# Hybrid decoder layer on one core: the residual reload ahead of a wait, sums of squares in column quarters, inverse roots spread by transposes

## The chip, the cores and the metric

The kernel runs on one core of a Trainium2 chip. The metric is the device time of one execution in microseconds (us). It is 1467.88 us, the median of three runs (1467.37 to 1468.05).

## The reference

One decoder layer over 1024 tokens of width 1024, with 16 learned meta tokens ahead of them, all in float32:

```python
u = rmsnorm(h, norm1_g)
proj = u @ w_in                        # q, k, v of 8 attention heads; q, f, i, g of 4 recurrent heads
o_sb = stick_breaking_attention(...)   # A[t,s] = sigmoid(z_ts) * prod_{s<j<t} (1 - sigmoid(z_tj))
o_sb = group_rmsnorm(merge_heads(o_sb), sb_norm_g, SB_HEADS)
o_hg = hgrn2_chunkwise(...)            # gated linear recurrence in chunks of 128
o_hg = group_rmsnorm(merge_heads(o_hg), hg_norm_g, HG_HEADS) * jax.nn.silu(hg_g)
h = h + jnp.concatenate([o_sb, o_hg], axis=-1) @ w_out
u2 = rmsnorm(h, norm2_g)
h = h + (jax.nn.silu(u2 @ w_gate) * (u2 @ w_up)) @ w_down
```

A last rmsnorm and the cut of the meta tokens follow. `group_rmsnorm` divides each head's output by the root of its mean square over the head's own width (64 in attention, 128 in the recurrence).

## The kernel before

Everything is written out by hand: each engine has its own instruction stream, and semaphores tie them. Large products are done with split operands: a float32 tensor is kept as a high part (fp32r) and a low part, and a product is three matmuls (high by high, high by low, low by high), lines 268 to 270 for results with features on the partitions and lines 280 to 282 for results with tokens on the partitions. The order of the stages is norm 1 and projections (to about 83 us), the recurrence of four heads (to about 351 us, `recurrence_tensor`), attention by four pairs of heads (to about 623 us, `attention_tensor`), the output projection with the residual sum and norm 2 (to about 746 us), and the FFN (to the end).

Head outputs lie with features on the partitions, so a head's mean square is a sum over partitions, and it is done on TensorE. Each half of a head (recurrence) or of a pair (attention) makes one group of four 128x128 tiles:

- Sums. ScalarE writes the squares; TensorE loads each tile of squares as weights and streams a column of ones (recurrence, `unit_sums`, line 576) or two columns that pick out the two heads of a pair (attention, `head_norm_tensor`, line 965). The result has tokens on the partitions.
- Roots. ScalarE takes the square root (line 979 in attention), VectorE inverts it and widens it to a tile (`widen`, and `head_norm_widen`, lines 986 and 988).
- Spread. TensorE loads the widened tile as weights and streams the identity (`unit_spread`, line 585, and line 971), which turns it so that tokens are on the columns. VectorE then scales `mixed` with it (line 807, and `head_norm_finish`, line 996).

There are 8 such groups in the recurrence and 8 in attention, so 16 groups of sums and 16 of spreads. The plain float32 matmuls of these lines appear as two instructions each in the trace.

Attention works on 56 pieces (14 for each pair of heads; a piece is a stretch of keys of one block of 128 queries). For each piece TensorE makes scores (lines 901 and 905), ScalarE two sigmoids (1029, 1032), VectorE a scan and a product (1084, 1091), TensorE turns the two heads' weights (917), two copies bring them out of PSUM, and TensorE multiplies by the values (936). The first head's copy is on ScalarE (line 1056). The second is on VectorE (line 1103) for pieces 0 to 41, and on ScalarE (line 1059) from piece 42, which is `SCALAR_COPIES`. In the last pair VectorE and ScalarE also split `mixed` into high and low parts (lines 1010 and 1015, at the pieces of `SPLIT_AT`; piece 53 is the last of them).

At the end of attention the last half goes out of PSUM (lines 1039 and 1040, semaphore `av_evac`), then through sums, root, spread, and scaling (semaphore `s_mixed`, value 8), while TensorE has begun the output projection. `out_group(c, t)` is 24 matmuls for column chunk `c` of 256 and token tile `t`; it uses one of four PSUM banks, so the fifth group waits for the first residual sum (`o_add`), and it also waits for the last split (`m_lo`, 16). The residual sum is `add` on VectorE (line 1351), into `h_res`, which is loaded again from `x` by GpSimd's queue. The queue's order is:

```python
pool.wait_ge(s_mixed.sem, s_mixed.done(8))
pool.dma_start(gain[:], norm2_g[0:1, :].to_broadcast([P, D])).then_inc(gain2.sem, 16)
pool.wait_ge(av_evac.sem, av_evac.done(8))
for t in range(TT):
    pool.dma_start(h_res[:, t, :], x2[t * P:(t + 1) * P, :]).then_inc(x_back.sem, 16)
```

`gain` shares its memory with the squares and the widened roots of attention. `h_res` lies over attention's inputs, which are no longer read once `av_evac` has its eighth count. VectorE waits for all eight tiles (`x_back` at 128) ahead of the first `add`.

Of the kernel before, what the change touches and what calls it, by code (L numbers as in the profile page):

```python
# [12 lines left out]
P = 128  # L13
# [5 lines left out]
TT = SEQ // P  # L19
# [57 lines left out]
PER_PAIR = len(PIECES) // 4  # L77
# [56 lines left out]
def hybrid_layer(nc, x, meta, norm1_g, w_in, sb_g, hg_g, lb_logits, w_out, norm2_g,  # L134
                 w_gate, w_up, w_down, final_g, out):
    x2, out2 = x[0], out[0]
# [7 lines left out]
    with ctx:  # L144
# [3 lines left out]
        def signal(name, credit=0):  # L148
            return Signal(ctx.enter_context(nc.semaphore(name)), credit)


        ident = sb("ident", [P, P])
        ident_bf = sb("ident_bf", [P, P], BF16)
        hidden_bf = sb("hidden_bf", [P, P], BF16)
        ones = sb("ones", [P, P])
        ones_pair = sb("ones_pair", [P, 2])
# [23 lines left out]
        with ExitStack() as heads:  # L180
# [7 lines left out]
            with ExitStack() as hg:  # L188
# [20 lines left out]
                scores = sb("scores", [P, U], stack=hg)  # L209
                kd_nat = sb("kd_nat", [P, U], stack=hg)  # L210
# [5 lines left out]
        squares, spread = gain[:, 0:HALF], gain[:, HALF:2 * HALF]  # L216
        gate_buf = (g_even[:], gain[:])

        with ExitStack() as ff:
# [5 lines left out]
            h_res = sb("h_res", [P, TT, D], stack=ff)  # L225
# [6 lines left out]
        def bank(n, w=HALF, rows=P):  # L232
            return ps[0:rows, n * HALF:n * HALF + w]
# [3 lines left out]
        META_COLS = slice(SEQ, L)  # L237
        MIX_HG = SB_WIDTH // P
        KEY_HALVES = [slice(0, P // 2), slice(P // 2, P)]
        UNITS = [(h, half) for h in range(HG_HEADS) for half in range(2)]  # L240


# [70 lines left out]
        av_done, av_evac = signal("av_done"), signal("av_evac")  # L313
# [1 line left out]
        s_inv, s_wide, s_spread = signal("s_inv"), signal("s_wide"), signal("s_spread")  # L315
        s_mixed = signal("s_mixed")
        m_hi, m_lo = signal("m_hi"), signal("m_lo")
        x_back, gain2, gain3 = signal("x_back"), signal("gain2"), signal("gain3")
        o_proj, o_add = signal("o_proj"), signal("o_add")
        came = {c: signal(f"w{c}_came") for c in "gud"}  # L320
        high = {c: signal(f"w{c}_high") for c in "gud"}
# [201 lines left out]
        def unit_scores(pe, n):  # L523
            head, half = UNITS[n]
            par = head % 2
# [46 lines left out]
        def unit_sums(pe, n):  # L572

            pe.wait_ge(h_square.sem, h_square.done(n + 1))
            for c in range(UNIT):
                last = nc.tensor.matmul(bank(4)[:, 2 * P + c:2 * P + c + 1],
                                        (kd_nat, scores)[n % 2][:, c * P:(c + 1) * P], ones[:, 0:1],
                                        start=True, stop=True)
            last.then_inc(h_sum.sem, 1)

        def unit_spread(pe, n):

            pe.wait_ge(h_wide.sem, h_wide.done(n + 1))
            for c in range(UNIT):
                last = nc.tensor.matmul(bank(1 + n % 2)[:, c * P:(c + 1) * P],
                                        (kd_nat, scores)[n % 2][:, c * P:(c + 1) * P], ident[:],
                                        start=True, stop=True)
            last.then_inc(h_spread.sem, 1)

        def meta_transpose(pe, head):  # L590
# [277 lines left out]


        NP = len(PIECES)  # L870
        SCALAR_COPIES = 3 * PER_PAIR

        def filling(n):

# [86 lines left out]
        def head_norm_tensor(pe, e, step, psum):  # L961
            if step == "sums":
                pe.wait_ge(s_square.sem, s_square.done(e + 1))
                for c in range(UNIT):
                    last = nc.tensor.matmul(psum[:, 2 * c:2 * c + 2], squares[:, c * P:(c + 1) * P],
                                            ones_pair[:], start=True, stop=True)
                last.then_inc(s_sum.sem, 1)
            else:
                pe.wait_ge(s_wide.sem, s_wide.done(e + 1))
                for c in range(UNIT):  # L970
                    last = nc.tensor.matmul(psum[:, c * P:(c + 1) * P], spread[:, c * P:(c + 1) * P], ident[:],
                                            start=True, stop=True)
                last.then_inc(s_spread.sem, 1)

        def head_norm_scalar(act, e, psum):
# [45 lines left out]
        def attention_scalar(act):  # L1021
            def sigmoids(n):
                pair, b, lo, hi, width, buf = PIECES[n]
                w, cols = hi - lo, place_of(n)
                act.wait_ge(z_done.sem, z_done.done(n + 1))
                if last_user(n) is not None:
                    act.wait_ge(t_done.sem, t_done.done(2 * last_user(n) + 2))
                for par in range(2):
                    nc.scalar.activation(beta[:, par, buf, cols], bank(2 * par + n % 2, w), ACT.Sigmoid,  # L1029
                                         scale=-SB_SCALE).then_inc(beta_done.sem, 1)  # L1030
                for par in range(2):
                    nc.scalar.activation(probs[:, par, buf, cols], bank(2 * par + n % 2, w), ACT.Sigmoid,
                                         scale=SB_SCALE).then_inc(sig_done.sem, 1)

            def out_evac(e):
                act.wait_ge(av_done.sem, av_done.done(e + 1))
                if e:
                    act.wait_ge(s_sum.sem, s_sum.done(e))
                nc.scalar.activation(squares, bank(5), ACT.Square).then_inc(s_square.sem, 1)
                nc.scalar.activation(mixed[:, e // 2, X_PARTS[e % 2]], bank(5), ACT.Copy).then_inc(av_evac.sem, 1)  # L1040

            def evacuate_filled(n):
                for j, u, piece in filling(n):
                    if piece != 0:
                        evacuate(act, j, u)

            evacuate(act, HG_HEADS + 1, "q0")
            act.wait_ge(h_mixed.sem, h_mixed.done(2 * HG_HEADS))
            sigmoids(0)
            sigmoids(1)  # L1050
            for n in range(NP):
                if n + 2 < NP:
                    sigmoids(n + 2)
                w = P * len(tiles_of(n))
                act.wait_ge(t_done.sem, t_done.done(2 * n + 1))
                nc.scalar.activation(probs_t[:, 0, 0:w], bank(4, w), ACT.Copy).then_inc(pt_first.sem, 1)
                if n >= SCALAR_COPIES:
                    act.wait_ge(t_done.sem, t_done.done(2 * n + 2))
                    nc.scalar.activation(probs_t[:, 1, 0:w], bank(6, w), ACT.Copy).then_inc(pt_second.sem, 1)
                if n in SUMS_AT:  # L1060
                    head_norm_scalar(act, SUMS_AT[n], bank(n % 2)[:, HALF - 8:HALF])
                evacuate_filled(n)
                if n - 1 in HALF_ENDS:
                    out_evac(HALF_ENDS.index(n - 1))
                for part in range(2):
                    if n - part in CHUNK_AT:
                        high_chunk(act, CHUNK_AT[n - part], None, part)
                for t, half in SPLIT_AT.get(n, []):
                    split_scalar(act, t, half)
            out_evac(7)  # L1070

        def attention_vector(dve):
# [24 lines left out]
            for n in range(NP):  # L1097
                w = P * len(tiles_of(n))
                if n in SPREAD_AT:
                    head_norm_finish(dve, SPREAD_AT[n], bank(7))  # L1100
                if n < SCALAR_COPIES:
                    dve.wait_ge(t_done.sem, t_done.done(2 * n + 2))
                    nc.vector.tensor_copy(probs_t[:, 1, 0:w], bank(6, w)).then_inc(pt_second.sem, 1)
                if n - 1 in SUMS_AT:
                    head_norm_widen(dve, SUMS_AT[n - 1])
                if n + 2 < NP:
                    weigh(n + 2)
                for part in range(2):
                    if n - 1 - part in CHUNK_AT:
                        low_chunk(dve, CHUNK_AT[n - 1 - part], part)  # L1110
                for t, half in SPLIT_AT.get(n, []):
                    split_vector(dve, t, half)


        with nc.Block() as blk:
# [45 lines left out]
            def _(pool):  # L1161
# [32 lines left out]
                for h in LEVELS[1:]:  # L1194
                    last = nc.gpsimd.memset(fac[h][:], 1.0)
                last.then_inc(fills.sem, 1)
                pool.wait_ge(s_mixed.sem, s_mixed.done(8))
                pool.dma_start(gain[:], norm2_g[0:1, :].to_broadcast([P, D])).then_inc(gain2.sem, 16)
                pool.wait_ge(av_evac.sem, av_evac.done(8))
                for t in range(TT):  # L1200
                    pool.dma_start(h_res[:, t, :], x2[t * P:(t + 1) * P, :]).then_inc(x_back.sem, 16)
                pool.wait_ge(n2.normed.sem, n2.normed.done(TT))
                pool.dma_start(gain[:], final_g.rearrange("(a n) -> a n", a=1).to_broadcast([P, D]))\
                    .then_inc(gain3.sem, 16)
# [104 lines left out]
            def _(dve):  # L1309
# [36 lines left out]

                def add(c, t):

                    dve.wait_ge(o_proj.sem, o_proj.done(TT * c + t + 1))
                    h = h_res[:, t, c * CW:(c + 1) * CW]  # L1350
                    nc.vector.tensor_tensor(h, h, bank(out_bank(c, t), CW), ALU.add).then_inc(o_add.sem, 1)  # L1351
# [3 lines left out]
                    hi_, lo_ = slot or ffn_slot(c)  # L1355
                    nc.vector.tensor_tensor(lo_, w_raw[:], hi_.bitcast(F32), ALU.subtract).then_inc(low[c].sem, 1)

                dve.wait_ge(x_back.sem, 16 * TT)
                for c in range(4):
                    for t in range(TT):  # L1360
                        add(c, t)
# [220 lines left out]
```

## Time and profile before

| | |
|---|---|
| median of three runs | 1467.88 us |
| profiled execution, its own time | 1466.36 us |
| its span, first to last instruction | 1464.3 us |
| TensorE busy, share of the span | 96% |
| VectorE, ScalarE, GpSimd busy | 50%, 30%, 1% |
| mean granted TensorE clock | 0.994 of full |
| chain of work that ended last: TensorE's share | 91% |

The trace is one execution. PE is TensorE's matmuls, PEld its weight loads, DVE is VectorE, ACT ScalarE, POOL GpSimd. L1351 is line 1351 of the kernel. Matmuls overlap each other in the pipeline, so the time from one start to the next says more than the duration of one. A query of the chain gives what each piece of time was waited on for; a query of waits gives idle time of an engine and who ended it.

### The profile page before, as it was taken

What the parts mean: (1) busy time and instruction counts of PE and PEld (TensorE: products, weight loads), DVE (VectorE), ACT (ScalarE), POOL (GpSimd) and SP (SyncE); (2) the same over time, 40 slices, a digit from 0 to 9 for tenths busy, and PEclk for the clock granted to TensorE, in tenths of its full rate; (3) what the DMA queues carried; (4) which work ended last, traced back from release to release, by engine and by line L of the source; (5) the groups of instructions that cost most, each with busy time, mean ns of one, the idle gap of its engine ahead of it and who ended that gap; (6) DMA issues with size and microseconds to landing.
All of it is one profiled execution on the core that took longest, in us unless ns stands there. A gap on an engine that the chain in (4) does not pass through costs nothing.

```text
span 1464.3 us, 20834 instructions
## 1 busy us (share of the span) xinstructions
PE 1401.8 (96%) x8732; PEld 1190.4 (81%) x8732; DVE 738.0 (50%) x1178; ACT 440.6 (30%) x770; POOL 20.3 (1%) x48
## 2 busy tenths in 40 slices
PE   5999999998999999769999999999999999999998
PEld 5898989897777777569987888888888888888886
DVE  6476677763776565812542435252533425152437
ACT  6323322223665556811432112111111112121113
POOL 3000000000000000010000000000000000000000
PEclk9999999999999999989999999999999999999999
DMA  6211111010010000040121011020201111020202
GB/s 189 58 30 30 30 30 53 22 44 0 1 59 1 30 2 30 1 158 30 58 73 58 29 58 58 29 87 0 86 23 63 31 55 57 29 86 0 86 0 115
DMA packets 61194, 68.78 MB, mean 47 GB/s; under 512 B 1584, under 2 KB 54832, under 8 KB 61120
## 3 DMA queue, kind: packets, MB, share of 16 engines
q1 hardware_dynamic: 59408, 61.94, 13.2%
q0 software_dynamic: 1712, 5.78, 1.1%
q8 instruction: 56, 0.92, 0.3%
q14 instruction: 18, 0.15, 0.0%
HBM read 63.51 MB, written 4.19 MB: 46 GB/s over the span
## 4 chain that ended last, share of the span: by engine, by line
PE 91%; ACT 5%; DMA 1%; issue 1%; DVE 1%; POOL 0%; ACTq 0%; DVEq 0%; POOLq 0%
PE ps L268 18%; PE ps L269 18%; PE ps L270 18%; PE ps L1542 16%; PE ps L936 3%; PE ps L917 2%; PE ps L280 2%; PE ps L282 2%; PE ps L281 2%; PE ps L901 2%; PE ps L549 2%; PE ps L384 1%; DMA h_res<-in_x_dram 1%; ACT bv L503 1%; ACT beta L1029 1%
## 5 line engine op out<-in xcount | busy, mean ns | idle before, releaser
L268 PE MATMUL ps<-a_hi,w_hi 128*128 128x512 f32 (+2 forms) x960 | 357.0, 372 | 8.5 <-DVE a_lo L376 2.9
L269 PE MATMUL ps<-a_lo,w_hi 128*128 128x512 f32 (+2 forms) x960 | 349.6, 364 | 0.0
L270 PE MATMUL ps<-a_hi,w_lo 128*128 128x512 f32 (+2 forms) x960 | 349.3, 364 | 0.0
L268 PEld LDWEIGHTS ps<-a_hi,w_hi 128*128 128x128 f32 x960 | 181.4, 189 | 33.8 <-DVE a_lo L376 3.3
L270 PEld LDWEIGHTS ps<-a_hi,w_lo 128*128 128x128 f32 x960 | 181.4, 189 | 23.4
L269 PEld LDWEIGHTS ps<-a_lo,w_hi 128*128 128x128 f32 x960 | 181.6, 189 | 22.1
L1386 DVE TENSOR_TENSOR silu<-silu,ps 128x512 f32<-128x512 f32 x44 | 30.2, 687 | 319.1 <-ACT silu L1272 319.1
L1398 DVE TENSOR_TENSOR h_res<-h_res,ps 128x512 f32<-128x512 f32 x176 | 116.3, 685 | 48.0 <-PE ps L1542 47.9
L1272 ACT ACTIVATE silu<-ps 128x512 f32<-128x512 f32 x44 | 26.4, 600 | 337.2 <-PE ps L270 337.2
L268 PE MATMUL ps<-a_hi,d_hi 128*128 128x512 f32 x320 | 124.5, 389 | 0.0
L269 PE MATMUL ps<-a_lo,d_hi 128*128 128x512 f32 x320 | 124.5, 389 | 0.0
L1542 PE MATMUL ps<-w_hi,f_hi 128*128 128x512 f32 x320 | 124.5, 389 | 0.0
L1542 PE MATMUL ps<-w_lo,f_hi 128*128 128x512 f32 x320 | 124.5, 389 | 0.0
L1542 PE MATMUL ps<-w_hi,f_lo 128*128 128x512 f32 x320 | 124.5, 389 | 0.0
L270 PE MATMUL ps<-a_hi,d_lo 128*128 128x512 f32 x320 | 124.5, 389 | 0.0
L1084 DVE TENSOR_TENSOR_SCAN beta<-beta,ones 128x272 f32<-128x272 f32 (+5 forms) x112 | 92.9, 871 | 15.8 <-ACT beta L1029 15.8
L1253 ACT ACTIVATE w_hi<-w_raw 128x2048 fp32r<-128x2048 f32 x22 | 42.2, 1920 | 167.0 <-DMA w_raw<-in_w_up_dram 67.7
L280 PE MATMUL ps<-w_hi,a_hi 128*128 128x256 f32 x256 | 74.1, 290 | 12.2 <-DVE h_res L1351 10.8
L435 DVE TENSOR_TENSOR w_lo<-w_raw,w_hi 128x2048 fp32r<-128x2048 f32 (+1 forms) x22 | 41.8, 1901 | 65.7 <-ACT w_hi L417 65.6
L281 PE MATMUL ps<-w_lo,a_hi 128*128 128x256 f32 x256 | 73.3, 286 | 0.0
L282 PE MATMUL ps<-w_hi,a_lo 128*128 128x256 f32 x256 | 73.3, 286 | 0.0
L268 PEld LDWEIGHTS ps<-a_hi,d_hi 128*128 128x128 f32 x320 | 60.2, 188 | 12.5
(193 smaller groups left out, 1959.8 us busy)
## 6 DMA issues: line engine op xcount, KB each, us to landing
w_raw<-in_w_in_dram SPq DMA_DIRECT2D x24, 512.0 KB
w_raw<-in_w_gate_dram SPq DMA_DIRECT2D x11, 1024.0 KB, 5.1
w_raw<-in_w_up_dram SPq DMA_DIRECT2D x11, 1024.0 KB, 5.2
w_raw<-in_w_down_dram SPq DMA_DIRECT2D x11, 1024.0 KB, 5.0
mixed<-in_x_dram SPq DMA_DIRECT2D x8, 512.0 KB, 7.3
w_raw<-in_w_out_dram SPq DMA_DIRECT2D x4, 1024.0 KB
h_res<-in_x_dram POOLq DMA_DIRECT2D x8, 512.0 KB, 8.0
out_dram<-h_sq SPq DMA_DIRECT2D x8, 512.0 KB, 2.6
```

What stands on the lines that cost most here:

```text
L268: nc.tensor.matmul(psum, wh, ah, start=k == 0, stop=False)
L269: nc.tensor.matmul(psum, wh, al, start=False, stop=False)
L270: last = nc.tensor.matmul(psum, wl, ah, start=False, stop=k == KT - 1)
L280: nc.tensor.matmul(psum, ah, wh, start=n == 0, stop=False)
L281: nc.tensor.matmul(psum, ah, wl, start=False, stop=False)
L282: last = nc.tensor.matmul(psum, al, wh, start=False, stop=n == KT - 1)
L435: last = nc.vector.tensor_tensor(w_lo[:, s, c], w_raw[:, c], w_hi[:, s, c].bitcast(F32), ALU.subtract)
L936: last = nc.tensor.matmul(dst, v, probs_t[:, par, i * P:(i + 1) * P], start=hi == width and i == 0, stop=lo == 0 and i == len(tiles) - 1)
L1084: nc.vector.tensor_tensor_scan(c, c, ones[:, 0:1].to_broadcast([P, hi - lo]), begin, ALU.mult, ALU.mult).then_inc(scanned.sem, 1)
L1253: nc.scalar.activation((slot or ffn_slot(c))[0], w_raw[:], ACT.Copy)\
L1398: nc.vector.tensor_tensor(h, h, bank(4 + g % 4), ALU.add).then_inc(dn_add.sem, 1)
L1542: last = nc.tensor.matmul(bank(4 + g % 4), fa[:, par, f, a], dw[:, w], start=f == 0 and m == 0, stop=f == 1 and m == 2)
```

## The change

There are five edits.

1. On GpSimd's queue the eight loads of `h_res` come first, behind `av_evac` alone; the gain of norm 2 comes behind them, after its wait for `s_mixed`.
2. `x_back` becomes one semaphore for each token tile, and `add(0, t)` waits for its own tile.
3. The sums of squares (both `unit_sums` and `head_norm_tensor`) are made by four matmuls for each tile in place of one: each loads 32 columns of the squares and writes 32 partitions of PSUM.
4. The spreads (both) are TensorE transposes in place of float32 matmuls by the identity.
5. `SCALAR_COPIES` becomes the range of pieces 42 to 53, so the second copies of pieces 54 and 55 go to VectorE.

```diff
+        QUARTERS = [slice(32 * i, 32 * i + 32) for i in range(4)]
@@
-        x_back, gain2, gain3 = signal("x_back"), signal("gain2"), signal("gain3")
+        x_back = [signal(f"x_back{t}") for t in range(TT)]
+        gain2, gain3 = signal("gain2"), signal("gain3")
@@ unit_sums
-                last = nc.tensor.matmul(bank(4)[:, 2 * P + c:2 * P + c + 1],
-                                        (kd_nat, scores)[n % 2][:, c * P:(c + 1) * P], ones[:, 0:1],
-                                        start=True, stop=True)
+                for rows in QUARTERS:
+                    last = nc.tensor.matmul(bank(4)[rows, 2 * P + c:2 * P + c + 1],
+                                            (kd_nat, scores)[n % 2][:, c * P + rows.start:c * P + rows.stop],
+                                            ones[:, 0:1], start=True, stop=True)
@@ unit_spread
-                last = nc.tensor.matmul(bank(1 + n % 2)[:, c * P:(c + 1) * P],
-                                        (kd_nat, scores)[n % 2][:, c * P:(c + 1) * P], ident[:],
-                                        start=True, stop=True)
+                last = nc.tensor.transpose(bank(1 + n % 2)[:, c * P:(c + 1) * P],
+                                           (kd_nat, scores)[n % 2][:, c * P:(c + 1) * P], ident[:])
@@
-        SCALAR_COPIES = 3 * PER_PAIR
+        SCALAR_COPIES = range(3 * PER_PAIR, NP - 2)
@@ head_norm_tensor
-                    last = nc.tensor.matmul(psum[:, 2 * c:2 * c + 2], squares[:, c * P:(c + 1) * P],
-                                            ones_pair[:], start=True, stop=True)
+                    for rows in QUARTERS:
+                        last = nc.tensor.matmul(psum[rows, 2 * c:2 * c + 2],
+                                                squares[:, c * P + rows.start:c * P + rows.stop],
+                                                ones_pair[:], start=True, stop=True)
@@
-                    last = nc.tensor.matmul(psum[:, c * P:(c + 1) * P], spread[:, c * P:(c + 1) * P], ident[:],
-                                            start=True, stop=True)
+                    last = nc.tensor.transpose(psum[:, c * P:(c + 1) * P], spread[:, c * P:(c + 1) * P], ident[:])
@@ attention_scalar
-                if n >= SCALAR_COPIES:
+                if n in SCALAR_COPIES:
@@ attention_vector
-                if n < SCALAR_COPIES:
+                if n not in SCALAR_COPIES:
@@ GpSimd's queue
+                pool.wait_ge(av_evac.sem, av_evac.done(8))
+                for t in range(TT):
+                    pool.dma_start(h_res[:, t, :], x2[t * P:(t + 1) * P, :]).then_inc(x_back[t].sem, 16)
                 pool.wait_ge(s_mixed.sem, s_mixed.done(8))
                 pool.dma_start(gain[:], norm2_g[0:1, :].to_broadcast([P, D])).then_inc(gain2.sem, 16)
-                pool.wait_ge(av_evac.sem, av_evac.done(8))
-                for t in range(TT):
-                    pool.dma_start(h_res[:, t, :], x2[t * P:(t + 1) * P, :]).then_inc(x_back.sem, 16)
@@ add(c, t)
+                    if c == 0:
+                        dve.wait_ge(x_back[t].sem, 16)
@@
-                dve.wait_ge(x_back.sem, 16 * TT)
```

## Rows read from the trace of the kernel before

**Rows 1.** Chain that ended last, 575 to 790 us: start, us, what

```profile
622.48 0.60 ACT mixed L1040
...
632.18 0.57 POOL gain L1198
632.75 3.65 POOL h_res L1201 x7
636.40 10.64 DMA h_res<-in_x_dram
```

**Rows 2.** Timeline of PE: start, us, engine line op out<-in tiles xcount [idle before <-releaser]

```profile
636.56 0.28 PE L282 MATMUL ps<-w_hi,a_lo 128*128 128x256 f32 x1
647.63 0.55 PE L280 MATMUL ps<-w_hi,a_hi 128*128 128x256 f32 x1 [10.79 <-DVE h_res L1351]
...
652.04 0.41 PE L282 MATMUL ps<-w_hi,a_lo 128*128 128x256 f32 x1
652.25 0.39 PE L280 MATMUL ps<-w_hi,a_hi 128*128 128x256 f32 x1
```

**Rows 3.** Busy by stage: PE, PEld, DVE, ACT, POOL, granted clock, DMA share, GB/s

```profile
647.00:655.00 8.00, 7.37 (x44) 7.40 (x44) 4.03 (x6) 0.00 (x0) 0.00 (x0) 0.66 0.38 131
```

**Rows 4.** Transfers of line 1201, whole span

```profile
DMA to landing us min/median/max: 5.4/8.0/10.6
```

**Rows 5.** Timeline of ACT and DVE after the last scaling

```profile
632.46 1.90 ACT L417 ACTIVATE w_hi<-w_raw 128x2048 fp32r<-128x2048 f32 x1
632.59 0.69 DVE L1015 TENSOR_TENSOR a_lo<-mixed,a_hi 128x512 fp32r<-128x512 f32 x1 [0.70 <-ACT a_hi L1010]
```

**Rows 6.** Timeline of PE, spread of the last half by float32 matmuls

```profile
630.04 1.06 PE L971 MATMUL ps<-ident,gain 128*128 128x128 f32 x8
...
630.86 0.36 PE L280 MATMUL ps<-w_hi,a_hi 128*128 128x256 f32 x1
```

**Rows 7.** Timeline of PE, eight transposes of norm 2

```profile
716.08 1.04 PE L384 MATMUL ps<-ident,h_norm 128*128 128x128 f32 x8
...
716.87 0.36 PE L280 MATMUL ps<-w_hi,a_hi 128*128 128x256 f32 x1
```

**Rows 8.** Timeline of PE, one group of sums in the recurrence

```profile
106.20 0.95 PE L576 MATMUL ps<-ones,kd_nat 128*128 128x1 f32 x8
...
107.01 0.40 PE L268 MATMUL ps<-a_hi,w_hi 128*128 128x336 f32 x1
...
107.25 0.32 PE L269 MATMUL ps<-a_lo,w_hi 128*128 128x336 f32 x1
```

**Rows 9.** Timeline of PE, one group of sums in attention

```profile
387.85 0.95 PE L965 MATMUL ps<-ones_pair,gain 128*128 128x2 f32 x8
388.73 0.30 PEld L901 LDWEIGHTS ps<-bf,bq 64*128 64x128 f32 x4
```

**Rows 10.** Timeline of PE, into column halves, through them, and out

```profile
83.27 0.60 PE L535 MATMUL ps<-ident,kd 128*128 128x128 f32 x4
83.80 1.09 PE L540 MATMUL ps<-bq,bk 128*64 128x128 f32 x16
84.72 0.64 PE L549 MATMUL ps<-mixed,bk 128*64 128x64 f32 x16
...
87.52 0.64 PE L549 MATMUL ps<-qd,kd 128*64 128x64 f32 x16
88.09 0.43 PE L268 MATMUL ps<-a_hi,w_hi 128*128 128x352 f32 x1
88.36 0.32 PE L269 MATMUL ps<-a_lo,w_hi 128*128 128x352 f32 x1
```

**Rows 11.** Chain that ended last, 585 to 623 us, its shares by line

```profile
by line: ACT a_hi L1010 18.9%; ACT probs_t L1059 13.5%; ACT beta L1029 13.4%; ACT probs_t L1056 11.8%; ACT probs L1032 10.6%; PE ps L936 9.8%; issue 6.7%; PE ps L917 3.9%; ACT L979 3.4%; ACT L1029 3.4%; ACT mixed L1040 2.9%; ACT gain L1039 
```

**Rows 12.** Timeline of ACT and DVE, second copy of piece 54

```profile
617.97 0.68 DVE L1015 TENSOR_TENSOR a_lo<-mixed,a_hi 128x512 fp32r<-128x512 f32 x1
618.03 0.49 ACT L1059 ACTIVATE probs_t<-ps 128x384 f32<-128x384 f32 x1
```

## Prediction

> **What bounds the kernel now.** The page comes first: TensorE is busy for 96% of the span and holds 91% of the chain that ended last, so time can be won where TensorE stops or where its work can be made shorter. The waits come next. TensorE stops for long at one place only, between attention and the FFN, and the chain through it reads as one story. The last attention output leaves PSUM at 622.48 + 0.60 = 623.08; GpSimd's queue is still waiting for the scaled last half and issues the norm gain at 632.18, then eight reloads from 632.75, and the last reload takes 10.64 us to land, until 647.04 [rows 1]. TensorE's last matmul before the stop starts at 636.56, the next at 647.63 [rows 2]. Its start to start there is normally 0.12 us, so the stop costs 647.63 - 636.68 = 10.95 us. Behind it the 256-column matmuls start every 0.21 us until 652.25 [rows 2]: 256 columns in 0.213 us is the lower of TensorE's levels, 1.2 GHz, and the stage's mean granted clock is 0.66 [rows 3]. That stretch of 4.62 us holds some 22 matmuls, which at 0.12 us take 2.6 us, so the idle engine's fallen clock costs 2.0 us more. The stop is worth 13.0 us in all.
>
> **Edits 1 and 2, the reload.** The loads can now issue from about 623.3 instead of 632.75 [rows 1], 9.4 us earlier, without the gain ahead of them (0.57 us). The first landed in 5.4 to 8.0 us and the last in 10.6 us after a start 3.7 us behind the first [rows 1, 4], so the first tile is there at about 629 to 631 and the last at 623.3 + 3.7 + 10.6 = 637.6. VectorE is free for the first add when its last split ends, 632.59 + 0.69 = 633.28 [rows 5]. The add of tile 0 then ends near 633.8, and TensorE asks for it at 636.68: 2.9 us to spare. Behind it on VectorE stands the split of the next weight chunk, which waits for ScalarE until 632.46 + 1.90 = 634.36 [rows 5] and ends near 636.7; the adds of tiles 1 to 3 follow, and TensorE asks for tile 1's bank one group (24 x 0.12 = 2.88 us) later, at 639.6. Nothing else is late, so the full stop and the slow stretch go: **-13.0 us**. The nine POOL issues keep their order but one: the gain now waits behind the reloads for 632.18 as before, is as large as one of them (0.5 MB, 5.4 to 10.6 us), and is wanted by norm 2 only near 716 us [rows 7]. VectorE's new waits by tile have a landed tile behind each. If the reload still came too late it would be by its last tile alone, 637.6 + 0.6 - 636.68 = 1.5 us of stop; I take 0.
>
> **Edit 4, transposes.** The spread of four tiles by float32 matmuls is eight instructions and takes 630.86 - 630.04 = 0.82 us [rows 6]. Eight transposes of the same tile size take 716.87 - 716.08 = 0.79 us [rows 7], and here eight instructions do eight tiles. Four will take about 0.42 with the 0.02 us that their first load starts late. Each group gets 0.40 us shorter. Of 16 groups, those of the recurrence (8) are all in TensorE's chain; of attention's 8, six are: from 585 to about 613 us the chain is ScalarE's [rows 11], and two spreads fall into it, where TensorE's time is not what is waited for. 14 x 0.40 = **-5.6 us**. The row of norm 2 is the same operation on the same tiles, so the bounds are close: 12 groups (-4.8) to all 16 (-6.4).
>
> **Edit 3, quarters.** Before, a group of sums has eight loads of 128 columns and takes 107.01 - 106.20 = 0.81 us up to the next matmul, whose successor comes after 0.24 us where 0.16 is normal for this width; 0.89 us with that [rows 8]. In attention it is 388.73 - 387.85 = 0.88 [rows 9]. The streams are one or two columns, so the load sets the 0.11 us between starts. Afterwards there are 16 matmuls, in float32 thus 32 instruction pairs, of 32 columns each. Two things have to be priced.
> Entering and leaving a narrower division of the array: the last full-width matmul starts at 83.27 + 3 x 0.11 = 83.61, and the first pair in halves at 83.80, where 0.11 later was due: 0.08 us, and a little more because the load no longer runs beside a matmul; I take 0.10. At the exit the last half starts at about 87.94 and the next at 88.09, 0.15 us, and the one behind it is late again (0.27 for 0.16), 0.11 us [rows 10]. In attention the score matmuls behind the sums use another division already, so that exit costs 0.18 before and after.
> The pair itself: in halves, 96 pairs go from 84.72 to 87.52, 0.029 us each, with 64 columns loaded and 64 streamed [rows 10]. That is the nearest row and the upper bound if nothing but width counts; the lower bound is the load alone with four quarters side by side, 0.112 / 4 / 4 = 0.007. I take 0.029, since nothing in the trace issues pairs faster.
> A group then costs 0.10 + 31 x 0.029 + 0.15 + 0.11 = 1.26 us in the recurrence (+0.37) and 0.10 + 0.90 + 0.18 = 1.18 in attention (+0.30). Eight of the first kind and seven of the second are in the chain (the eighth lies in the stretch that is ScalarE's): 3.0 + 2.1 = **+5.1 us**. At 0.007 it would be 8 x (0.58 - 0.89) + 7 x (0.50 - 0.88) = -5.1. The turning point is 0.018 us a pair.
> The Trainium skill's page TensorEngine Tiling (Array Packing), Instruction Overhead, speaks against this edit: a matmul costs about 60 cycles however few columns stream, and one should not tile a dimension that is already small. Its page TensorE: Matmul & The Clock Gate, in the part on 56 ns, puts the least start to start at about 25 ns; by that the quarters would cost +3.2 us and the sum would come 1.9 us lower. No row here streams fewer than 64 columns in a divided array, so the trace does not decide it.
>
> **Edit 5, the copies.** ScalarE's second copy of piece 54 ends at 618.03 + 0.49 = 618.52. VectorE is in the split of `mixed` until 617.97 + 0.68 = 618.65 [rows 12], so its copy ends about 0.49 later, 619.14, and TensorE's value matmuls and everything to the end of attention wait for it: **+0.6 us**. Were VectorE free, it would cost nothing; piece 55 is such a case, with a copy that starts and ends as before. Bounds 0 to 0.7.
>
> **The sum.** -13.0 - 5.6 + 5.1 + 0.6 = -12.9 us. Against the profiled execution (1466.36, of which 1464.3 is span) that is 1453.5; that execution was 1.5 us below the median of the runs, and the forecast for the median is 1467.88 - 12.9 = **1455.0 us**.
>
> **The rivals.**
> (a) Quarters are cheap: the pairs are not bound by the row of the halves, whose 64 streamed columns at 2.4 GHz alone take 27 ns. Then a pair costs 0.007 to 0.018 us, and the sum is 1467.88 - 13.0 - 5.6 + 0.6 - (0 to 5.1) = 1444.8 to 1449.9. For it: the halves' row is exactly its streaming time, so the load is not what limits it. Against it: 32 pairs are 64 instructions, and no row shows two instructions in less than 0.029. The page TensorE: Matmul & The Clock Gate of the Trainium skill, in the part on packing, gives about 4 ns from tile to tile, which is this rival.
> (b) A new wait stands in place of the stop: the reload's tiles land together at the end, or the split of the last half comes late because sums of 1.2 us lie ahead of it (slack 636.68 - 633.28 = 3.4 us, of which they take 0.3). That leaves 1.5 us of stop, and, if the clock falls again behind it, 2.0 us more: 1456.5 to 1458.5.
> (c) Slower than before: a 32-column load costs as much as a 128-column one, 0.112 us, and quarters are not taken side by side. The 15 groups in the chain then cost 465 x (0.112 - 0.029) = 38.6 us more than forecast, 1493.6. The point from which it decides is a pair of 0.029 + 12.9 / 465 = 0.057 us, which is what the halves take with 128 columns streamed (0.92 / 16 from 83.80 to 84.72) [rows 10]. Against it: the 0.029 of the halves is already far below.
>
> **How the numbers follow.** Forecast 0.60, (a) 0.28, (b) 0.09, (c) 0.03. The likeliest time is 1455.0, with its own range 1452 to 1457. For 8 times in 10 the range has to reach into (a), whose ends are even: 1446 to 1458. About 0.2% (2.9 us) is what a measurement of this kernel can tell from no change. All cases but (c) are faster by more: faster 0.96, same 0.01, slower 0.03.
>
> **What would show it.** In the changed kernel's profile: no wait of line 280 for `h_res`, the reload issued near 623, and a granted clock of 1.00 where it was 0.66; four instructions for a spread and about 0.42 us; 32 for a group of sums, whose start to start decides between forecast and (a) (above or below 0.018); the copy of piece 54 on VectorE starting at the end of the split of line 1015. Wrong would be: a stop of TensorE after the fourth group of the output projection, a spread of eight instructions, or a pair interval outside 7 to 29 ns.

## The result and the profile after

The changed kernel takes 1444.41 us (median of 4 runs, 1443.5 to 1445.05) where the kernel before takes 1467.62 (4 runs): a ratio of 0.9842, 95% interval 0.9825 to 0.9859, or 23.2 us less. Forecast were 12.9 us less and a range from 1446 to 1458. The result lies below the range, beside the lower end of rival (a).

The two profiled executions took 1466.36 and 1445.05 us, 21.3 us apart; the stages below are theirs. Five marks divide the span, each the start of an instruction: the first matmul of the recurrence's levels (line 549 before), the first scores of attention (line 901 before), the last copy out of attention's PSUM (line 1040 before), the first transposes of norm 2, and the end.

| stage, us | before | after | saved | forecast |
|---|---|---|---|---|
| norm 1 and projections, to line 549 | 84.7 | 85.6 | -0.9 | 0 |
| recurrence | 269.0 | 262.6 | 6.4 | 0.2 |
| attention | 268.8 | 267.0 | 1.8 | -0.4 |
| output projection, to norm 2's first transposes | 93.6 | 79.7 | 13.9 | 13.1 |
| norm 2 and the FFN | 748.2 | 748.2 | 0.0 | 0 |

(The last half of attention has its sums and its spread in the output projection; the forecast column is split that way.) No edit touches the first stage; in the other traces it takes 83.8 to 85.1 us. The reload came out as forecast. The surprise is in the recurrence.

First the reload. GpSimd's queue after (timeline; start, us, engine line, operation, idle before):

```profile
616.02 4.22 POOL L1202 DMA_DIRECT2D h_res<-in_x_dram  x8 [572.60 <-ACT mixed L1043]
624.03 0.53 POOL L1204 DMA_DIRECT2D gain<-in_norm_g_dram  x1 [3.79 <-DVE mixed L999]
```

The eight reloads issue right behind attention's last copy, and the gain behind them once the last half is scaled. On VectorE:

```profile
624.44 0.69 DVE L1018 TENSOR_TENSOR a_lo<-mixed,a_hi 128x512 fp32r<-128x512 f32 x1 [0.70 <-ACT a_hi L1013]
625.05 0.41 DVE L1356 TENSOR_TENSOR h_res<-h_res,ps 128x256 f32<-128x256 f32 x1
```

The first residual sum follows the last split without a gap, 9 us after the first reload was issued. By stages (PE, PEld, DVE, ACT, POOL busy, granted clock, DMA share, GB/s), where before stood [rows 3]:

```profile
616.00:632.00 16.00, 16.00 (x161) 15.85 (x162) 5.99 (x10) 3.73 (x4) 4.75 (x9) 1.00 0.90 339
632.00:695.00 63.00, 63.00 (x527) 63.00 (x526) 16.94 (x28) 8.65 (x9) 0.00 (x0) 1.00 0.15 50
```

TensorE is busy for 15.85 of the first 16 us and without a hole behind them, at full clock, although the DMA engines are 90% busy in the first. The stop of [rows 2] is gone, and no wait for `h_res` is left.

Now a group of sums in the recurrence, which answers to [rows 8] (PE's timeline):

```profile
106.88 0.32 PE L271 MATMUL ps<-a_hi,w_lo 128*128 128x352 f32 x1
107.13 0.43 PE L579 MATMUL ps<-ones,kd_nat 128*32 128x1 f32 x32
107.50 0.42 PE L269 MATMUL ps<-a_hi,w_hi 128*128 128x336 f32 x1
107.76 0.32 PE L270 MATMUL ps<-a_lo,w_hi 128*128 128x336 f32 x1
```

32 pairs take 107.50 - 107.13 = 0.37 us, way out included. The forecast had them at 0.90 without it. From the due start (106.88 + 0.16 = 107.04) to the second matmul behind it is 0.72 us; before, 106.20 to 107.25, it was 1.05. So the group got 0.33 us shorter where 0.37 longer was forecast. In attention:

```profile
382.15 0.32 PE L271 MATMUL ps<-a_hi,w_lo 128*128 128x336 f32 x1
382.40 0.43 PE L968 MATMUL ps<-ones_pair,gain 128*32 128x2 f32 x32
382.76 0.94 PE L903 MATMUL ps<-bf,bq 64*128 64x400 f32 x4
```

From the matmul ahead to the scores is 0.61 us, against 388.73 - 387.70 = 1.03 before ([rows 9]; the matmul ahead of that group started at 387.70): 0.42 less. The spread of the last half is four instructions and 0.36 us, against 0.82 in [rows 6]:

```profile
622.35 0.60 PE L975 MATMUL ps<-ident,gain 128*128 128x128 f32 x4
622.71 0.36 PE L281 MATMUL ps<-w_hi,a_hi 128*128 128x256 f32 x1
```

By these rows and the forecast's count of groups attention should have gained 6 x 0.42 + 5 x 0.40 = 4.5 us. It gained 1.8. Two questions were open: what a pair of quarters costs and why, and where 2.7 us of attention went.

### The profile page after: what moved, and what is told of

Read it like the earlier page. It is cut to its first block, busy times and chain, and to the rows that moved or that the text cites. A ratio compares the mean times of both kernels' runs of the same rounds, so it can differ in the third digit from the quotient of the medians.

```text
span 1443.0 us, 21481 instructions
## 1 busy us (share of the span) xinstructions
PE 1389.1 (96%) x9052; PEld 1172.3 (81%) x9052; DVE 739.0 (51%) x1180; ACT 439.2 (30%) x768; POOL 19.5 (1%) x48
## 3 DMA queue, kind: packets, MB, share of 16 engines
q1 hardware_dynamic: 59408, 61.94, 13.2%
## 4 chain that ended last, share of the span: by engine, by line
PE 93%; ACT 4%; DVE 1%; issue 1%; DMA 1%; ACTq 0%; DVEq 0%; POOLq 0%
PE ps L269 19%; PE ps L271 18%; PE ps L270 18%; PE ps L1546 17%; PE ps L938 3%; PE ps L919 3%; PE ps L281 2%; PE ps L283 2%; PE ps L282 2%; PE ps L903 2%; PE ps L551 2%; PE ps L386 1%; ACT bv L505 1%; PE ps L542 1%; DMA gain<-in_norm_g_dram 1%
## 5 line engine op out<-in xcount | busy, mean ns | idle before, releaser
L270 PE MATMUL ps<-a_lo,w_hi 128*128 128x512 f32 (+2 forms) x960 | 349.7, 364 | 0.0
L271 PEld LDWEIGHTS ps<-a_hi,d_lo 128*128 128x128 f32 x320 | 60.2, 188 | 12.6
```

The lines of the kernel that those rows point to most:

```text
L270: nc.tensor.matmul(psum, wh, al, start=False, stop=False)
L271: last = nc.tensor.matmul(psum, wl, ah, start=False, stop=k == KT - 1)
```

## The experiments

### One edit at a time

All four ran on one chip beside 25 runs of the kernel before (median 1466.60).

**Edits 1 and 2 alone.** (The lines of the queue; the semaphores by tile are those of the change.)

```diff
+                pool.wait_ge(av_evac.sem, av_evac.done(8))
+                for t in range(TT):
+                    pool.dma_start(h_res[:, t, :], x2[t * P:(t + 1) * P, :]).then_inc(x_back[t].sem, 16)
                 pool.wait_ge(s_mixed.sem, s_mixed.done(8))
```

> The kernel before with edits 1 and 2 alone (the reload first on GpSimd's queue, a semaphore for each tile). Theory (the stop of TensorE was a wait for the reload, and its slow stretch came with it): 13.0 us less than before, no wait of line 280 for h_res, granted clock 1.00 where it was 0.66. Rival (a new wait takes the stop's place): 9 to 11 us less.

Measured: 1453.29, ratio 0.9911 (0.9890 to 0.9931), 13.3 us less. The output projection is 13.2 us shorter in the trace (79.6 against 92.8 from its first matmul), all other stages as before, and TensorE has neither a stop nor a low clock:

```profile
636.00:656.00 20.00, 20.00 (x169) 20.00 (x169) 4.43 (x10) 1.92 (x1) 0.00 (x0) 1.00 0.23 80
```

This term of the sum is right. The stop and the low clock behind it went together, so the split into 11.0 and 2.0 us was not tested by itself.

**Edit 3 alone.** (Attention's lines; the recurrence's change likewise.)

```diff
-                last = nc.tensor.matmul(psum[:, 2 * c:2 * c + 2], squares[:, c * P:(c + 1) * P], ...)
+                for rows in QUARTERS:
+                    last = nc.tensor.matmul(psum[rows, 2 * c:2 * c + 2],
+                                            squares[:, c * P + rows.start:c * P + rows.stop], ...)
```

> The kernel before with edit 3 alone. Theory A (a pair of quarters costs 0.008 us, as the changed kernel's trace has it): a group in the recurrence is 0.33 us shorter from the matmul ahead of it to the second behind it (0.88 for 1.21), one in attention 0.42, so 8 x 0.33 + 7 x 0.42 = 5.6 us less. Theory B (the forecast on record, 0.029 us a pair): 5.1 us more. Theory C: TensorE is freed but not the chain in attention, so only the recurrence's 2.6 us come through.

Measured: 1461.80, ratio 0.9970 (0.9958 to 0.9982), 4.8 us less. The forecast's +5.1 falls. The ten runs lie in two groups, 1460.05 to 1460.76 and 1462.84 to 1465.39, with the median between them, so the 4.8 is rough; the same edit undone, further down, costs 4.9. In the trace (a run of the lower group) the recurrence is 3.2 us shorter and attention 1.7. The last group, which lies in the output projection, brings nothing here: TensorE's wait for `h_res` stands behind it and is 11.07 us for 10.79.

**Edit 4 alone.**

```diff
-                last = nc.tensor.matmul(..., spread[:, c * P:(c + 1) * P], ident[:], start=True, stop=True)
+                last = nc.tensor.transpose(..., spread[:, c * P:(c + 1) * P], ident[:])
```

> The kernel before with edit 4 alone. Theory: 14 of 16 groups, 0.40 us each, 5.6 us less. Rival (shorter work in attention makes TensorE idle more where ScalarE sets the pace, and its clock falls there): 3.2 us less from the recurrence, and at most 1 us from attention, with stretches at granted clock 0.5 that the kernel before has not.

Measured: 1462.13, ratio 0.9966 (0.9956 to 0.9976), 4.5 us less. In the trace it is 3.6 in the recurrence and 1.4 in attention, and again nothing in the output projection. That is between theory and rival, and the trace has one stretch of low clock in attention.

**Edit 5 alone.**

```diff
-        SCALAR_COPIES = 3 * PER_PAIR
+        SCALAR_COPIES = range(3 * PER_PAIR, NP - 2)
```

> The kernel before with edit 5 alone. Theory (the forecast on record): the copy of piece 54 starts behind the split of line 1015 and ends 0.6 us later; 0.6 us more in all. Rival (as in the changed kernel's trace, VectorE is through with the split in time): 0.0 us.

Measured: 1468.15, ratio 1.0007 (0.9996 to 1.0017): not told from no change, and not from the 0.6 us forecast. In the profiled execution the copy of piece 54 starts at the end of the transposes it copies (timeline):

```profile
618.83 0.87 PE L917 MATMUL ps<-ident,probs 128*128 128x128 f32 x6
618.89 0.68 DVE L1015 TENSOR_TENSOR a_lo<-mixed,a_hi 128x512 fp32r<-128x512 f32 x1
619.41 0.49 ACT L1056 ACTIVATE probs_t<-ps 128x384 f32<-128x384 f32 x1 [1.02 <-PE ps L917]
619.74 0.56 DVE L1103 COPY probs_t<-ps 128x384 f32<-128x384 f32 x1 [0.17 <-PE ps L917]
620.44 0.88 PE L936 MATMUL ps<-probs_t,bv 128*64 128x128 f32 x12 [0.74 <-DVE probs_t L1103]
```

VectorE is through with the split (619.57) before the transposes end. In [rows 12] it was the other way round: the split ended at 618.65, behind the transposes. What shifted TensorE against VectorE by about 1 us lies 6 us earlier, ahead of anything the edit touches, and is a fall of the clock. It is taken up below.

### What a pair costs

These three ran on another chip, beside the kernel before at 1467.27 (7 runs; 1467.62 in the result), and are set against the changed kernel's 1444.4.

**Full-width sums in the changed kernel** (edit 3 undone).

```diff
-                for rows in QUARTERS:
-                    last = nc.tensor.matmul(bank(4)[rows, 2 * P + c:2 * P + c + 1], ...)
+                last = nc.tensor.matmul(bank(4)[:, 2 * P + c:2 * P + c + 1], ...)
```

> The changed kernel with edit 3 undone (full-width sums). Theory A (quarters save 5 to 6 us): 1449 to 1450, against 1444.4 with quarters. Theory B (quarters cost 5.1 us): 1439. If some of attention's saving is lost to ScalarE's pace, 1447 to 1449.

Measured: 1449.27, ratio 0.9881 (0.9864 to 0.9897): 4.9 us above the changed kernel. So quarters are worth about the same with the other edits as without them.

**Halves in place of quarters.**

```diff
-        QUARTERS = [slice(32 * i, 32 * i + 32) for i in range(4)]
+        QUARTERS = [slice(64 * i, 64 * i + 64) for i in range(2)]
```

> The changed kernel with the sums in column halves (64 columns, 16 pairs for a group) in place of quarters. Theory A (loads of different column parts run side by side, so a pair costs its columns over the number of parts: 0.112 / 2 / 2 = 0.028 us): 16 x 0.028 = 0.45 us for a group where quarters take 0.25; 3 us more than the changed kernel for 15 groups, 1447. Theory D (a pair has a price of its own near 0.008 us, whatever its width): 16 x 0.008 = 0.13 us, 1.8 us less than the changed kernel, 1442.6.

Measured: 1444.71, ratio 0.9849 (0.9832 to 0.9865). The total misses theory A's 1447; the rows do not:

```profile
105.70 0.63 PE L579 MATMUL ps<-ones,kd_nat 128*64 128x1 f32 x16
106.27 0.42 PE L269 MATMUL ps<-a_hi,w_hi 128*128 128x336 f32 x1
```

16 pairs take 0.63 with the last matmul's own 0.20 in it: (0.63 - 0.20) / 15 = 0.029 us a pair. The recurrence is 263.8 us in its trace, 1.2 more than with quarters, where 8 x 0.20 = 1.6 was due. Attention took 266.3, less than the changed kernel's 267.0. It had one stretch of low clock there and the changed kernel three, and what those cost is measured below.

This is the measurement that the prediction lacked. The halves of [rows 10] load 64 columns and stream 64; here they load 64 and stream one, and the pair costs the same 0.029. So the load by itself is enough to set that row: 0.11 us for 128 columns, half of it for 64, and half again, which fits two parts of the array that load side by side. It does not follow that the stream had no limit there. The first pairs of [rows 10] load the same 64 columns and stream 128, and take 0.057, twice as long for twice the stream; at 64 columns the two limits fall together. That is why the row could not tell what a pair with one streamed column costs.

**Every quarter matmul twice.**

```diff
-                for rows in QUARTERS:
+                for rows in QUARTERS * 2:
```

> The changed kernel with each quarter matmul of the sums done twice, one set behind the other in each tile (64 pairs for a group where 32 were). It prices the pair by itself, without entry and exit. Theory A (0.008 us a pair): 15 groups x 32 x 0.008 = 3.8 us more than the changed kernel, 1448.2. Theory B (0.029): 13.9 us more, 1458.

Measured: 1448.27, 3.9 us above the changed kernel, where 0.008 us a pair gives 3.8 and 0.029 gives 13.9. The row:

```profile
106.19 0.71 PE L579 MATMUL ps<-ones,kd_nat 128*32 128x1 f32 x64
106.84 0.42 PE L269 MATMUL ps<-a_hi,w_hi 128*128 128x336 f32 x1
```

64 pairs take 0.65 us, 32 take 0.37: 0.28 / 32 = 0.009 us a pair, and 0.09 for the way out. The forecast's lower bound, 0.112 / 4 / 4 = 0.007, is nearly reached. Each pair is two instructions, so TensorE goes through 64 of them in 0.28 us, which answers the forecast's doubt whether instructions can follow each other so fast.

### Where attention's 2.7 us went

**Edit 5 undone in the changed kernel.**

```diff
-        SCALAR_COPIES = range(3 * PER_PAIR, NP - 2)
+        SCALAR_COPIES = 3 * PER_PAIR
```

> The changed kernel with edit 5 undone (the second copies of pieces 54 and 55 on ScalarE). Forecast on record: 0.6 us less than the changed kernel. Rival (VectorE is ahead of TensorE by then): no difference, 1444.4.

Measured: 1444.29, beside the changed kernel's 1444.41 on another chip: no difference. By the medians the copies are not where the gain went.

The clock is part of it. In the changed kernel's trace the granted clock is below 1.00 in three short stretches of attention, in the kernel before's in none. Two of them:

```profile
495.00:500.00 5.00, 5.00 (x28) 3.34 (x30) 0.30 (x1) 1.48 (x3) 0.00 (x0) 0.66 0.02 7
...
601.00:606.00 5.00, 4.37 (x30) 3.33 (x28) 5.00 (x9) 4.23 (x10) 0.00 (x0) 0.66 0.01 3
```

A mean of 0.66 over 5 us is 3.4 us at the lower level, 1.2 GHz. Ahead of the first, TensorE was busy for 0.62 of 2.5 us:

```profile
492.50:495.00 2.50, 0.62 (x6) 0.38 (x4) 2.45 (x5) 2.45 (x5) 0.00 (x0) 1.00 0.77 268
```

and ahead of the one near 601 for 0.52 of 2.5, while ScalarE and VectorE, which set the pace of the last pair, were busy throughout:

```profile
598.50:601.00 2.50, 0.52 (x4) 0.42 (x4) 2.47 (x6) 2.49 (x7) 0.00 (x0) 1.00 0.00 0
```

Such a stretch is not enough for a fall. The kernel before has the same one at the same place in the work, and its clock stays at 1.00:

```profile
500.50:503.00 2.50, 0.62 (x7) 0.38 (x5) 2.29 (x4) 2.45 (x5) 0.00 (x0) 1.00 0.76 270
```

**The kernel before, once more.**

> The kernel before, once more, for its clock. Its trace has no fall of the granted clock in attention, the changed kernel's has three of 3.4 us. If the shorter work of edits 3 and 4 makes the clock fall, this execution has none again, and attention takes 268.7 to 268.9 us. If the falls come and go by themselves, it may have one or two, with 1 to 2 us more in attention.

Measured, in one run: 1465.68; attention 268.7 us and no fall in it, as the first time.

**ScalarE and VectorE relieved.** The high and low parts of the recurrence's half of `mixed` go to GpSimd, ahead of the reload on its queue (cut; the splits that stay with ScalarE and VectorE begin at a later piece):

```diff
+                for i, (t, half) in enumerate(POOL_SPLITS):
+                    nc.gpsimd.tensor_copy(tok_hi[:, t, X_PARTS[half]], mixed[:, t, X_PARTS[half]])...
+                    nc.gpsimd.tensor_tensor(tok_lo[:, t, X_PARTS[half]], mixed[...], tok_hi[...], ALU.subtract)...
                 pool.wait_ge(av_evac.sem, av_evac.done(8))
```

> The changed kernel with the eight splits of the recurrence's half of mixed (high and low part, 16 instructions of 128x512) taken from ScalarE and VectorE and given to GpSimd, ahead of the reload on its queue. Theory (in the last pair of attention ScalarE and VectorE set the pace, and TensorE's savings there come to nothing): ScalarE loses 8 x 0.51 = 4.1 us of work in that stretch and VectorE 8 x 0.64 = 5.1, so attention's stage is 3 to 4 us shorter, 1441. Rival (GpSimd's work slows VectorE or ends after the last attention output, so that the output projection waits for it): no gain, or 2 us and more lost.

Measured: 1447.41 (ratio 0.9874, 0.9858 to 0.9890), 3 us worse than the changed kernel; attention is 269.7 for 267.0. The theory's 3 to 4 us did not come, as its rival had it, and the test of the theory is spoilt by a side effect: while GpSimd worked, VectorE got slow. The product of line 1094 (1095 here) on 383 columns, from 569 to 590 us, first with the splits on GpSimd, then in the changed kernel:

```profile
L1095 DVE TENSOR_TENSOR probs<-probs,beta 128x383 f32<-128x383 f32 x4 | 4.9, 1256 | 0.0
```

```profile
L1094 DVE TENSOR_TENSOR probs<-probs,beta 128x383 f32<-128x383 f32 x4 | 2.0, 542 | 0.0
```

In this trace the clock also fell for 6.8 us from 599.1, twice as long as near there in the changed kernel, so not all of the loss need be VectorE's.

**TensorE kept busy.** 82 small matmuls fill its idle time in the last pair:

```diff
+                if n == 52:
+                    keep_busy(n, 28)
@@ behind turn(n)
+                keep_busy(n, {45: 10, 47: 10, 48: 10, 49: 8, 50: 8, 51: 8}.get(n, 0))
```

> The changed kernel with small idle-time matmuls (bf16, 128x128, into an unused bank, results never read) on TensorE in the last pair of attention: 8 or 10 behind the transposes of pieces 45 and 47 to 51, and 28 ahead of the spread of piece 52, 82 in all. Theory (attention gave back its saving because the clock fell while TensorE waited for ScalarE there): the falls near 578 and 601 are gone, attention is 1 to 2 us shorter than the changed kernel's 267.0, 1443. Rival (what was given back went to ScalarE's pace alone, and the falls cost nothing): 1444.4, or up to 2 us more by the added matmuls.

**The changed kernel beside it.**

> The changed kernel again, beside the one with the idle-time matmuls: 1444.4 by its earlier runs, and two or three falls of the clock in attention if these belong to the changed kernel; none or one if they come and go.

Measured, 5 runs each on one chip: 1443.48 (1442.41 to 1445.46) with the added matmuls, 1444.39 (1443.16 to 1445.30) without. The ranges overlap, so a gain is not shown. The falls near 578 and 601 are gone in the trace with the added matmuls:

```profile
575.00:613.00 38.00, 30.47 (x348) 22.26 (x348) 35.10 (x57) 32.35 (x73) 0.00 (x0) 1.00 0.01 2
```

and in the changed kernel's second profile they are there again (575.0 and 598.9), the clock of the same stretch at 0.91:

```profile
575.00:612.00 37.00, 28.36 (x266) 19.00 (x264) 33.10 (x53) 31.41 (x70) 0.00 (x0) 0.91 0.01 1
```

The execution without falls in the last pair also shows edit 5's cost at last. TensorE is not late there, the copy of piece 54 waits for VectorE's split (line 1030 in this kernel, from 608.43 to 609.11), and the value matmuls come 609.72 - 607.45 = 2.27 us behind the transposes, not 1.61 as above:

```profile
607.45 0.88 PE L919 MATMUL ps<-ident,probs 128*128 128x128 f32 x6
...
609.03 0.55 DVE L1118 COPY probs_t<-ps 128x384 f32<-128x384 f32 x1
609.72 0.88 PE L938 MATMUL ps<-probs_t,bv 128*64 128x128 f32 x12 [1.39 <-DVE probs_t L1118]
```

That is 0.66 us for the 0.6 forecast. In these traces edit 5 costs its price when TensorE is in time, and less or nothing when the clock has made TensorE late (0.2 in the execution with halves).

What a fall costs can be read without a model, since the same work is found in every trace. The second profile of the changed kernel has no fall near 496, and the first has. ScalarE's first sigmoid of piece 34, in the kernel before, in the changed kernel and in the changed kernel again (timeline):

```profile
510.49 0.69 ACT L1029 ACTIVATE beta<-ps 128x272 f32<-128x272 f32 x2 [0.20 <-PE ps L901]
503.81 0.69 ACT L1032 ACTIVATE beta<-ps 128x272 f32<-128x272 f32 x2 [0.21 <-PE ps L903]
500.59 0.69 ACT L1032 ACTIVATE beta<-ps 128x272 f32<-128x272 f32 x2 [0.20 <-PE ps L903]
```

Counted from attention's first scores (353.67, 348.12 and 346.35) these are 156.82, 155.69 and 154.24 us: saved are 1.13 in one and 2.58 in the other. At piece 32, ahead of the fall, both had saved 2.6. So this fall cost 1.45 us. The table has the same difference at more places: the time saved against the kernel before at the first sigmoid of a piece, and at the last copy.

| execution | low clock in attention: start (3.4 us each unless said) | piece 32 | piece 34 | piece 48 | piece 54 | last copy |
|---|---|---|---|---|---|---|
| kernel before again | none | 0.0 | 0.0 | 0.0 | 0.1 | 0.1 |
| edits 1 and 2 | none | 0.0 | 0.0 | 0.0 | 0.1 | 0.1 |
| edit 3 alone | 602.7 | 1.7 | 1.7 | 2.6 | 2.6 | 1.7 |
| edit 4 alone | 602.7 | 0.9 | 0.9 | 1.8 | 1.8 | 1.4 |
| edit 5 alone | 503.9, 609.8 | 0.0 | -1.5 | -1.5 | -1.4 | -2.3 |
| changed kernel | 496.1, 578.0, 601.9 | 2.6 | 1.1 | 2.9 | 2.8 | 1.8 |
| changed kernel again | 349.7, 575.0, 598.9 | 2.6 | 2.6 | 4.3 | 4.2 | 3.4 |
| with added matmuls | 494.2 | 2.6 | 1.1 | 2.8 | 2.9 | 2.2 |
| edit 5 undone | 494.1, 576.0, 599.9 (6.8 us) | 2.6 | 1.1 | 2.9 | 2.5 | 0.5 |
| halves | 599.9 | 1.8 | 1.8 | 3.2 | 3.2 | 2.5 |
| full-width sums | 579.2 (6.8 us) | 0.9 | 0.9 | 1.8 | 0.3 | 0.3 |
| every quarter twice | 498.3, 580.2, 604.1 (6.8 us) | 1.5 | 0.0 | 1.2 | 0.8 | -1.3 |

(The execution with GpSimd's splits also had three falls, but its VectorE was slower besides.)

Three things can be read from it.

- The edits bring nearly what the rows promised. Where no fall came near 496, 4.3 us are saved by piece 48, against the 4.5 of the sum. Sums save 0.42 to 0.44 in each of six groups; of the spreads ahead of the last pair four save 0.39 to 0.50 each, and the first, near 393 in the trace of edit 4 alone, saves nothing.
- The fall near 496 took 1.45 us of it, the fall near 578 took 0.1 by piece 54, and 1.0 went between piece 54 and the last copy, where the third fall lies. 4.3 - 1.45 - 0.1 - 1.0 = 1.8 us. But a fall is not the only thing that can cost in the last stretch: with the added matmuls, without a fall there, it costs 0.66, by edit 5's copy. Without falls the changed kernel would have saved about 3.7 by this reckoning, not 4.3.
- What a fall costs depends on where it comes. The one near 579 in the execution with full-width sums, twice as long, cost 1.5 by piece 54, the short one at 578.0 in the changed kernel 0.1. In the changed kernel's second profile the one at 349.7 comes where TensorE waits for ScalarE anyway, and by piece 8 it has cost 0.05. A fourth fall there, from 612.5, comes behind the last copy, and the output projection takes 81.1 us for 79.7.

This is also why the added matmuls brought so little. They removed falls that cost about 1 us together, edit 5's 0.66 came in their place, and attention, 266.6 us, kept its fall near 494. The theory's 1 to 2 us were not there to be had.

Why the clock falls in one execution and not in the next stays open. All profiles with edit 3 or 4 have at least one fall in attention, and three executions whose attention is the kernel before's (two of that kernel, one with edits 1 and 2) have none. But the execution with edit 5 alone had two, at places that come before anything it changes. Shorter sums and spreads may make them more frequent, which is not shown; they are not needed for one.

## Why the prediction was wrong

- **The stop and its slow stretch, -13.0.** Right: -13.3 with these edits alone. Nothing was late in the stop's place, and rival (b) did not come.
- **Transposes, -5.6.** Instruction count and saving for each group (0.40 forecast, 0.46 in the last row) right. Alone they measured -4.5. In that trace the recurrence gave 3.6 for the 3.2 forecast. Attention gave 1.8 by piece 48 and 1.4 at its end for the 2.0 forecast: the first spread saved nothing, and 0.45 went between piece 54 and the last copy, where the clock fell. The last group's 0.4 could not show while the stop stood behind it.
- **Quarters, +5.1.** This is the step that failed, in its size and so in its sign. Alone it is -4.8, and undoing it costs 4.9. The term that was mis-sized is the pair, 0.029 forecast and 0.009 measured; 465 intervals x 0.020 = 9.3 us, nearly the whole error of 10.3 in the total. The cost of entering and leaving (0.36 with both sides) was 0.09 + 0.09 + 0.10 = 0.28. The wrong choice was in "I take 0.029, since nothing in the trace issues pairs faster": the row bore on a pair with four times the load work, since twice the columns go to half as many parts. That the row also equalled its own streaming time, as the prediction says under (a), should have told that it could not say what limits a pair that streams one column.
- The Trainium skill's least start to start of about 25 ns (TensorE: Matmul & The Clock Gate, the part on 56 ns) is not borne out here: 9 ns for pairs in four column parts. The prediction also misread the Trainium skill's page TensorEngine Tiling (Array Packing), Instruction Overhead, as speaking against the edit. It says not to tile a dimension that is already small; what is small here is the stream, and what was tiled are the 128 columns that are loaded. The statement that bears on it is in Tiling Modes, on the same page of the Trainium skill: different tiles can load and multiply in parallel. The 0.11, 0.029 and 0.009 us agree with it for the loads.
- **Copies, +0.6.** Right as a mechanism (0.66 in the execution where TensorE is in time), but it is there only then; the medians, 1444.29 without the edit and 1444.41 with it, do not show it.
- **The range.** Rival (a) had 1444.8 as its end, and the result is 0.4 below that; the range stopped at 1446 because (a) was taken as even between its ends, although its lower end was simply the load rate. The bound was nearly right and the weight wrong. That it is met so closely is in part luck: the transposes gave less than forecast, and the reload a little more.
- **The clock in attention** was not in the forecast at all. In the profiled execution of the changed kernel attention saved 1.8 us where about 3.7 were due without falls.
- **The edits together.** Alone they measured 13.3 + 4.8 + 4.5 = 22.6 us, with the copies at nothing; together 23.2. The last group's sums and spread are in the output projection, and there they count only when the stop is gone: the stage is 13.9 us shorter in the changed kernel and 13.2 with edits 1 and 2.

## What to carry to other kernels

A matmul whose moving side is a column or two costs what its weight load costs; here, with the stationary side cut into four column quarters, 32 pairs took 0.37 us with the way out, where 8 full-width pairs took 0.81. Before a row of the trace is used as a price, ask which of its two halves (load or stream) set it: in halves, a pair that loads 64 columns and streams 64 could not tell. When a saving seems to vanish, compare the same instruction in two executions of the same kernel, as at piece 34; it shows where the time went without a model. A reload should wait only for the reader that frees its buffer, not for later work that happens to stand ahead in its queue: that alone was 13.3 of 23.2 us.

## What the runs showed of the hardware

- Start to start of float32 load-and-matmul pairs with one or two columns streamed: 0.11 us at 128 columns loaded, 0.029 in halves of 64, 0.009 in quarters of 32. The step from full width to halves is a factor of about 4, to quarters about 12.
- TensorE's granted clock fell for 3.4 us at a time (6.8 in some) in attention, twice right behind 2.5 us in which TensorE was busy for 0.52 to 0.62; the kernel before had such a stretch and no fall. One and the same kernel had a fall near 496 in one execution and not in the next. A fall cost 1.45 us there, and 0.05 where TensorE waited anyway.
- While GpSimd did copies and subtractions on 128x512 tiles, a VectorE product took 1256 ns for 542.
